# Gate products in fp32r with 256 moving columns a token, four tokens to a block of two weight units, and a reordered early gelu on ScalarE

## The chip, the cores and the metric

One Trainium2 chip, one of its cores. The kernel is a single program with one instruction stream for each engine: TensorE (PE, with its weight loads shown apart as PEld), VectorE (DVE), ScalarE (ACT), GpSimd (POOL) and SyncE (SP). The metric is the device time of one execution in microseconds, the median over several runs.

## The reference

Two blocks of a model on one sequence of 256 tokens with 2048 features, in fp32. The first is an attention and convolution block with a gated embedding. The second is a recurrent branch, a sparse attention branch and then the part that matters here, a layer of 16384 experts (128 by 128 keys):

```python
q = (xf @ wq).reshape(t, PEER_HEADS, PEER_QDIM)
...
top_s, pos = lax.top_k(cand_s, PEER_TOPK)
expert = jnp.take_along_axis(cand_i, pos, axis=-1).reshape(t, -1)
gate = jax.nn.softmax(top_s.astype(jnp.float32), axis=-1).astype(x.dtype).reshape(t, -1)
...
z = jnp.einsum('cd,ced->ce', xc, u[ec])
act = jax.nn.gelu(z, approximate=False) * gc
return jnp.einsum('ce,ced->cd', act, v[ec])
```

Each token picks 128 of the 16384 experts (8 heads, 16 each). The kernel doesn't gather them. It computes z for all experts, multiplies gelu(z) by a gate that is zero where the token didn't pick the expert, and multiplies the result by all of v.

## The kernel before, in words

**Weights in units.** All large weights come in one stream of 904 units of 128 by 1024 fp32 (512 KB), two units to a pair, four buffers (`raw`, `w_hi`, `w_lo`). SyncE loads a unit (L565), ScalarE rounds it to fp32r (`split_hi`, L460), VectorE subtracts to get the rest (`split_lo`, L469). A product is then taken as high times high, high times low and low times high in fp32r. Both splits are written as `ahead(...)`: in the turn of pair p they are made for pair p + 2, and the split of unit u of that pair waits until TensorE has finished unit u of pair p (`unit_done`), because it takes over that unit's buffer.

**A pair of u** (128 experts, one block of z): `halves_out` on TensorE does, for each of the two units, eight matmuls of w_hi with 512 columns (L509, both halves of the activations) and eight of w_lo with 256 columns (L514). The two halves of the bank are then added. Every one of the 128 blocks of z passes through ScalarE's gelu. There are 64 "early" blocks, whose gelu is kept in HBM (`z_kept`) since the gates aren't there yet, and 64 "late" ones.

**Stages of this layer**, in TensorE's order:
- `wqu`, 8 turns of 4 pairs: two of the query projection, two of u. The early blocks go through `early` (L986 to L994) on ScalarE: copy the bank to SBUF (L984), wait until GpSimd has added the halves (L634), gelu (L991), store to `z_kept` (L993).
- `u_decode`, 16 pairs of u, while VectorE works out the picked experts and their gates. At its end three transposes bring the first index, the second index and the gate of each token's 128 picks to partitions (`slot_t`, copied by L1032).
- `u_gates`, 32 pairs of u, with the gate matrix G (second index by first index by token, 128 KB a partition) made between them. For each token, GpSimd writes a one-hot tile of the second index (L655), VectorE one of the first index times the gate (L1787), and TensorE multiplies them in plain fp32 with 128 columns (L2224; the trace holds two matmul records a token). Four tokens follow each unit; ScalarE copies their bank to G (`keep_gates`, L1041). `low_half` (L520) and `add_halves` (L525) put z together, then gelu (L1053) and the store (L1055).
- `u_late`, 64 pairs of u: `low_half`, `add_halves`, gelu (L1071), then on VectorE the gate product of this late block (L1802) and of one early block (L1805) that ScalarE's queue has brought back from `z_kept` (L1064).
- `v`, 128 pairs: 24 matmuls of 512 columns a pair (L2249 to L2251). The expert activations are split two blocks ahead (`expert_hi` L1076, `expert_lo` L1809).

**What sets the order in `u_gates`.** Every engine works through its own instructions in order. On VectorE that order is, for each unit, four tiles (L1787), `split_lo` of one unit, and behind the second unit `add_halves`. On ScalarE: `split_hi` of unit 0, `keep_gates(0)`, `split_hi` of unit 1, `low_half`, `keep_gates(1)`, gelu, store. The tiles are single buffers for each of four tokens, handed back by `hot_used`.

Of the kernel before, what the change touches and what calls it, by code (L numbers as in the profile page):

```python
# [70 lines left out]
         ("wqu", 4 * PH), ("u_decode", 2 * PH), ("u_gates", S // 8), ("u_late", NB // 2), ("v", NB)]  # L71
EARLY = NB // 2
# [11 lines left out]
for _name, _count in [("conv", 4 * CONV_J), ("rnn", 2 * KT), ("heads", 2 * H2), ("u_gates", S // 8),  # L84
                      ("u_late", NB // 2)]:
    HALVED[_name] = _n
    _n += _count
# [46 lines left out]
def build(nc, stream, x, p_t, rows, consts, params, rg_w, ukv, keys_t, out):  # L134
    ctx = ExitStack()
    with ctx:
# [26 lines left out]
        hot = sb("hot", [P, 2, 4, P])  # L163
# [107 lines left out]

        GZ = c("band").rearrange("p (s n) -> p s n", s=2)
# [156 lines left out]
        hot_used = [sem(f"hot_used{n}") for n in range(4)]  # L429
        gate_kept = [sem(f"gate_kept{n}") for n in range(2)]  # L430
# [69 lines left out]
        def halves_out(pe, pair, odd, bank, units=(0, 1), fills=None):  # L500
# [97 lines left out]
        def _(pool):  # L598
# [49 lines left out]
            with pool.Fori(0, S // 8) as i:  # L648
                pool.wait_ge(hot2, i * 8 + 1)
                pool.tensor_copy(idx8, slot_t[:, 1, bass.ds(i * 8, 8)]).then_inc(g_step, 1)  # L650
                pool.wait_ge(g_step, i + 1)
                for s in range(8):
                    pool.wait_ge(hot_used[s % 4], i * 2 + s // 4 + 1)
                    pool.sem_inc(hot_turn, 1)
                    pool.tensor_scalar(hot[:, 1, s % 4, :], iota, idx8[:, s:s + 1], None, ALU.is_equal)\  # L655
                        .then_inc(hot2, 1)
# [9 lines left out]
        def _(act):  # L666
# [319 lines left out]
            def early(pair, b2, n, block, before):  # L986

                copy_halves(Z_HALVES[:, n, :], banks[2 + n], pair, block, before)
                act.wait_ge(z_saved[n], b2 * 16 + 1)
# [7 lines left out]
            with act.Fori(0, PH) as h:  # L997
# [10 lines left out]
                keep_query(0)  # L1008
                ahead(split_hi, act, "wqu", h, 4, 1)
# [3 lines left out]
                early(pair_of("wqu", h, 4, 2), h, 0, h * 4 + 2, 4)  # L1013
                keep_scores(1)
                ahead(split_hi, act, "wqu", h, 4, 3)
                early(pair_of("wqu", h, 4, 3), h, 1, h * 4 + 3, 4)
# [13 lines left out]
            for a in range(3):  # L1030
                act.wait_ge(picks_turned, 2 * a + 2)
                act.activation(slot_t[:, a, :], banks[4 + a][:, 0:S], ACT.Copy).then_inc(slots_kept, 1)  # L1032
            early_turn(PH - 1)
            act.wait_ge(slots_kept, 3)
            act.wait_ge(x_saved, 16)

            with act.Fori(0, S // 16) as i:
                for n in range(2):
                    def keep_gates(m):
                        act.wait_ge(hot_used[3], i * 4 + 2 * n + m + 2)  # L1040
                        act.activation(G[:, :, bass.ds(i * 16 + (8 * n + 4 * m), 4)],  # L1041
                                       banks[m][:, :].rearrange("p (t b) -> p b t", t=4), ACT.Copy)\
                           .then_inc(gate_kept[m], 1)

                    ahead(split_hi, act, "u_gates", i, 2, n, units=(0,))
                    keep_gates(0)
# [4 lines left out]
                    keep_gates(1)  # L1051
# [26 lines left out]
            with act.Fori(0, EARLY // 2 - 1) as i:  # L1078
                late_turn(i)
# [3 lines left out]
            late_turn(EARLY // 2 - 1)  # L1083
            for n in range(2):
                act.wait_ge(act_ready[n], EARLY // 2 + 1)
                act.wait_ge(early_ready[n], EARLY // 2 + 1)
# [5 lines left out]
            with act.Fori(0, NB // 2 - 8) as i:  # L1092
                next_experts(i)
# [47 lines left out]
        def _(dve):  # L1141
# [639 lines left out]
            dve.wait_ge(slots_kept, 3)  # L1781
            with dve.Fori(0, S // 16) as i:
                for n in range(2):
                    for s in range(8):
                        tok = i * 16 + (8 * n + s)
                        dve.wait_ge(hot_used[s % 4], i * 4 + (2 * n + s // 4) + 1)
                        dve.tensor_scalar(hot[:, 0, s % 4, :], iota, slot_t[:, 0, bass.ds(tok, 1)],  # L1787
                                          slot_t[:, 2, bass.ds(tok, 1)], ALU.is_equal, ALU.mult).then_inc(hot1, 1)
                        if s % 4 == 3:
                            ahead(split_lo, dve, "u_gates", i, 2, n, units=(s // 4,))  # L1790
                    add_halves(dve, GZ[:, n, :], banks[2 + n], block_of("u_gates", i, 2, n))
            for n in range(2):
                dve.wait_ge(gate_kept[n], S // 8 + 1)
# [18 lines left out]
            with dve.Fori(0, EARLY // 2 - 1) as i:  # L1812
                late_turn(i)
# [3 lines left out]
            late_turn(EARLY // 2 - 1)  # L1817
            for n in range(2):
                dve.wait_ge(act_ready[n], EARLY // 2 + 1)
                dve.wait_ge(early_ready[n], EARLY // 2 + 1)  # L1820
            with dve.Fori(0, NB // 2 - 2) as i:
                for n in range(2):
                    ahead(split_lo, dve, "v", i, 2, n)
                    expert_lo(i * 2 + (2 + n), n, i * 2 + (3 + n))
# [50 lines left out]
        def _(pe):  # L1875
# [339 lines left out]
            with pe.Fori(0, S // 16) as i:  # L2215
                for n in range(2):
                    pe.wait_ge(gelu_ready[n], i + (2 * PH + 1))
                    for m in range(2):
                        halves_out(pe, pair_of("u_gates", i, 2, n), n, banks[2 + n], units=(m,))
                        pe.wait_ge(gate_kept[m], i * 2 + n + 1)  # L2220
                        for s in range(4):
                            pe.wait_ge(hot1, i * 16 + (8 * n + 4 * m + s + 1))
                            pe.wait_ge(hot2, i * 16 + (8 * n + 4 * m + s + 1) + 1)
                            pe.matmul(banks[m][:, s * P:(s + 1) * P], hot[:, 1, s, :], hot[:, 0, s, :], start=True,  # L2224
                                      stop=True).then_inc(hot_used[s], 1)

            with pe.Fori(0, EARLY // 2) as i:
# [4 lines left out]
            def expert(i, n, first=False):  # L2232
                pe.wait_ge(el_ready, i * 2 + n + 1)
                if first:
                    for m in range(2):
                        pe.wait_ge(gate_kept[m], S // 8 + 1)
                for u in range(2):
                    if first and u == 1:
                        wait_summed(pe, block_of("u_late", EARLY // 2 - 1, 2, 1))
# [159 lines left out]
```

## Time and profile before

| | us |
|---|---|
| median of 3 runs (2788.06 to 2791.62) | 2789.57 |
| the profiled execution, its own time | 2789.84 |
| its span | 2787.9 |
| TensorE matmul busy | 2744.4 |
| TensorE weight loads busy | 2366.5 |
| VectorE busy | 1818.3 |
| ScalarE busy | 1409.1 |
| GpSimd busy | 342.3 |
| mean granted TensorE clock, share of full | 0.996 |

A matmul's record is longer than the time that it adds, since matmuls overlap. So what a group of matmuls costs is read from where one group starts to where the next starts. The same holds for VectorE and ScalarE instructions that follow each other without a wait.

### The profile page before, as it was taken

How to read it: one execution, taken by the hardware profiler on the slowest of the kernel's cores; microseconds unless marked ns; L12 is line 12 of the kernel's file. 1: busy time of each engine (PE TensorE's matmuls, PEld its weight loads, DVE VectorE, ACT ScalarE, POOL GpSimd, SP SyncE). 2: the span in 40 equal slices, each digit the busy share in tenths (PEclk: the TensorE clock that was granted, in tenths of full speed). 3: DMA queues.
4: the chain of work that ended last, by engine and by line, in shares of the span. 5: the costliest groups of instructions: out<-in, count | busy, mean ns of one | idle time of the engine just before them, and what ended most of it. 6: DMA issues, size and time to landing. Idle time of an engine off the chain costs nothing.

```text
span 2787.9 us, 48242 instructions
## 1 busy us (share of the span) xinstructions
PE 2744.4 (98%) x14688; PEld 2366.5 (85%) x14688; DVE 1818.3 (65%) x2903; ACT 1409.1 (51%) x2067; POOL 342.3 (12%) x438
## 2 busy tenths in 40 slices
PE   8999999999999999999999999999999999999998
PEld 6888878888888888888888999888888888888887
DVE  6666665668986666579995666666665555555555
ACT  5455545556665444466655544555554444444444
POOL 0000000000001110011126996000000000000000
PEclk9999999999999999999999999999999999999999
DMA  6544455564554444555555445666665555555564
GB/s 244 190 156 162 150 169 187 177 218 159 173 179 160 158 155 140 195 183 192 191 195 176 156 158 162 214 214 209 214 206 196 195 190 195 192 192 195 191 238 158
DMA packets 153554, 514.76 MB, mean 185 GB/s; under 512 B 17056, under 2 KB 33696, under 8 KB 152480
## 3 DMA queue, kind: packets, MB, share of 16 engines
q1 hardware_dynamic: 131904, 480.44, 52.2%
q10 hardware_dynamic: 21600, 33.70, 3.4%
q8 instruction: 26, 0.43, 0.1%
q14 instruction: 24, 0.20, 0.0%
HBM read 501.49 MB, written 12.58 MB: 184 GB/s over the span
## 4 chain that ended last, share of the span: by engine, by line
PE 73%; issue 21%; POOL 2%; DVE 2%; ACT 1%; DMA 0%; POOLq 0%; SPq 0%; DVEq 0%; ACTq 0%
PE bank L509 21%; PE bank L514 11%; PE bank L2249 8%; PE bank L2251 8%; PE bank L2250 8%; PE bank L547 3%; PE bank L549 3%; PE bank L548 3%; PE bank L2224 2%; POOL big L634 2%; DVE w_lo L469 1%; PE bank L492 1%; PE bank L494 1%; PE bank L493 1%; PE bank L2082 0%
## 5 line engine op out<-in xcount | busy, mean ns | idle before, releaser
L469 DVE TENSOR_TENSOR w_lo<-raw,w_hi 128x1024 fp32r<-128x1024 f32 x904 | 1105.7, 1236 | 796.2 <-ACT w_hi L460 791.0
L460 ACT ACTIVATE w_hi<-raw 128x1024 fp32r<-128x1024 f32 x904 | 951.4, 1059 | 933.0 <-PE bank L2251 373.2
L509 PE MATMUL bank<-act,w_hi 128*128 128x512 f32 x3840 | 980.7, 397 | 5.4 <-ACT big L984 1.9
L509 PEld LDWEIGHTS bank<-act,w_hi 128*128 128x128 f32 x3840 | 692.0, 189 | 136.2 <-issue 7.8
L514 PEld LDWEIGHTS bank<-act,w_lo 128*128 128x128 f32 x3840 | 523.3, 190 | 39.4 <-DVE w_lo L469 0.8
L514 PE MATMUL bank<-act,w_lo 128*128 128x256 f32 x3840 | 535.1, 282 | 0.1
L2249 PE MATMUL bank<-w_hi,expert_act 128*128 128x512 f32 x1008 | 392.2, 389 | 0.1
L2250 PE MATMUL bank<-w_lo,expert_act 128*128 128x512 f32 x1008 | 392.1, 389 | 0.0
L2251 PE MATMUL bank<-w_hi,expert_act 128*128 128x512 f32 x1008 | 392.1, 389 | 0.0
L2249 PEld LDWEIGHTS bank<-w_hi,expert_act 128*128 128x128 f32 x1008 | 189.3, 188 | 39.6 <-DVE cst L525 0.5
L2251 PEld LDWEIGHTS bank<-w_hi,expert_act 128*128 128x128 f32 x1008 | 189.3, 188 | 39.3
L2250 PEld LDWEIGHTS bank<-w_lo,expert_act 128*128 128x128 f32 x1008 | 189.3, 188 | 39.2
L655 POOL TENSOR_SCALAR hot<-cst,stat 128x128 f32<-128x128 f32 x256 | 211.2, 841 | 15.9 <-PE bank L2224 8.7
L661 POOL TENSOR_TENSOR big<-big 128x1024 f32<-128x1024 f32 x2 | 5.8, 2876 | 1051.0 <-DVE big L1836 1051.0
L547 PE MATMUL bank<-w_hi,act 128*128 128x512 f32 x320 | 126.1, 394 | 2.1 <-DVE act L1376 0.9
L548 PE MATMUL bank<-w_lo,act 128*128 128x512 f32 x320 | 125.2, 391 | 0.0
L549 PE MATMUL bank<-w_hi,act 128*128 128x512 f32 x320 | 125.1, 391 | 0.0
L634 POOL TENSOR_TENSOR big<-big 128x256 f32<-128x256 f32 x48 | 61.4, 1280 | 321.6 <-ACT big L984 321.6
L1787 DVE TENSOR_SCALAR hot<-cst,slot_t 128x128 f32<-128x128 f32 x256 | 78.1, 365 | 0.0
L547 PEld LDWEIGHTS bank<-w_hi,act 128*128 128x128 f32 x320 | 60.4, 189 | 16.2 <-DVE w_lo L469 1.5
L1071 ACT ACTIVATE cst<-cst 128x256 f32<-128x256 f32 x64 | 26.8, 419 | 92.7 <-DVE cst L525 92.7
L619 POOL TENSOR_TENSOR big<-big 128x256 f32<-128x256 f32 x16 | 11.2, 699 | 497.3 <-DVE big L525 497.3
(308 smaller groups left out, 2603.3 us busy)
## 6 DMA issues: line engine op xcount, KB each, us to landing
raw<-in_stream SPq DMA_DIRECT2D x904, 512.0 KB, 3.3
big<-in_ukv ACTq DMA_DIRECT2D x16, 512.0 KB, 4.6
z_kept<-cst ACTq DMA_DIRECT2D x64, 128.0 KB, 3.1
cst<-z_kept ACTq DMA_DIRECT2D x64, 128.0 KB, 3.8
big<-in_x SPq DMA_DIRECT2D x2, 1024.0 KB, 9.6
big<-in_rows ACTq DMA_DIRECT2D x2, 1024.0 KB, 8.3
big<-in_rg_w ACTq DMA_DIRECT2D x1, 2048.0 KB, 11.0
x_kept<-big ACTq DMA_DIRECT2D x1, 2048.0 KB, 6.7
```

Of the source, the lines that this page charges most:

```text
L460: act.activation(w_hi[:, s, :], raw[:, s, :], ACT.Copy).then_inc(hi_ready, 1)
L469: dve.tensor_tensor(w_lo[:, s, :], raw[:, s, :], w_hi[:, s, :].bitcast(F32), ALU.subtract).then_inc(lo_ready, 1)
L509: pe.matmul(bank[:, :], w_hi[:, s, kk * P:(kk + 1) * P], act2[:, k, :, :].rearrange("p a n -> p (a n)"), start=(k == 0), stop=False)
L514: mm = pe.matmul(bank[:, 0:S], w_lo[:, s, kk * P:(kk + 1) * P], act_hi[:, k, :], start=False, stop=(k == KT - 1))
L547: pe.matmul(outs[t], a_hi, hi, start=(k == 0), stop=False)
L548: pe.matmul(outs[t], a_hi, lo, start=False, stop=False)
L549: mm = pe.matmul(outs[t], a_lo, hi, start=False, stop=(k == KT - 1))
L634: pool.tensor_tensor(dest, halves[:, 0:S], halves[:, S:2 * S], ALU.add).then_inc(pool_summed, 1)
L655: pool.tensor_scalar(hot[:, 1, s % 4, :], iota, idx8[:, s:s + 1], None, ALU.is_equal)\
L2249: pe.matmul(o, a_hi, hi, start=first, stop=False, skip_group_check=True)
L2250: pe.matmul(o, a_hi, lo, start=False, stop=False, skip_group_check=True)
L2251: mm = pe.matmul(o, a_lo, hi, start=False, stop=False, skip_group_check=True)
```

## The change

- The gate product of a token becomes one fp32r matmul of 256 columns: the one-hot tile of the second index (exact in fp32r) times a tile that holds, side by side, the first index's one-hot times the rounded gate and times the gate's rest. The result is two halves, low and high, which must be added.
- `u_gates` now has 64 pairs and four tokens a pair instead of 32 pairs and eight. `u_late` has 32 pairs instead of 64. So 96 blocks of z are early and 32 late; the 64 early blocks that `u_late` no longer brings back are brought back and multiplied in the first turns of `v`.
- TensorE does the four tokens between the w_hi and the w_lo matmuls of the pair's second unit (`between`).
- VectorE makes the four double tiles first, with one `scalar_tensor_tensor` of 128 by 256 each, then both `split_lo`, then `add_halves`, and then adds the high half of the gates from PSUM onto G, in two instructions of 128 by 256 (`add_gates`).
- ScalarE copies the low half of the gates to G, in two instructions of 128 by 256, between its two `split_hi`.
- In `wqu` and `u_decode` the gelu and the store of an early block (`save_early`) stand behind the splits of the next pair.

```diff
+         ("wqu", 4 * PH), ("u_decode", 2 * PH), ("u_gates", S // 4), ("u_late", NB // 4), ("v", NB)]
+EARLY = 3 * NB // 4
+LATE = NB - EARLY
...
-        hot = sb("hot", [P, 2, 4, P])
+        weighted = sb("weighted", [P, 4, 2, P], F32R)
...
+        GATE_BANKS = [[banks[0], banks[1]], [banks[4], banks[5]]]
...
+                if u and between:
+                    between()
                 pe.wait_ge(lo_ready, 2 * pair + u + 1)
...
             def early_turn(i):
                 for n in range(2):
                     ahead(split_hi, act, "u_decode", i, 2, n)
-                    early(pair_of("u_decode", i, 2, n), i + PH, n, i * 2 + (4 * PH + n), 2)
+                    save_early(i + (PH - 1 + n), 1 - n, i * 2 + (4 * PH + n - 1))
+                    keep_early(pair_of("u_decode", i, 2, n), n, i * 2 + (4 * PH + n), 2)
...
                     ahead(split_hi, act, "u_gates", i, 2, n, units=(0,))
-                    keep_gates(0)
+                    for half in range(2):
+                        act.wait_ge(hot_used[2 * half + 1], i * 2 + n + 2)
+                        act.activation(G[:, :, bass.ds(i * 8 + (4 * n + 2 * half), 2)],
+                                       GATE_BANKS[n][half].rearrange("p (t a b) -> p a b t", t=2, a=2)[:, 1, :, :],
+                                       ACT.Copy).then_inc(gate_low, 1)
                     ahead(split_hi, act, "u_gates", i, 2, n, units=(1,))
...
-                    keep_gates(1)
...
+            with act.Fori(0, (EARLY - LATE) // 2) as i:
+                for n in range(2):
+                    act.wait_ge(early_ready[n], i + (LATE // 2 + 1))
+                    act.dma_start(GB[:, n, :], z_kept[bass.ds(i * 2 + (LATE + n), 1), :, :]
+                                  .rearrange("o p n -> (o p) n")).then_inc(z_back[n], 16)
+                next_experts(i)
...
+            def add_gates(i, n):
+                for half in range(2):
+                    dve.wait_ge(gate_low, i * 4 + (2 * n + half + 1))
+                    dest = G[:, :, bass.ds(i * 8 + (4 * n + 2 * half), 2)]
+                    high = GATE_BANKS[n][half].rearrange("p (t a b) -> p a b t", t=2, a=2)[:, 0, :, :]
+                    dve.tensor_tensor(dest, dest, high, ALU.add).then_inc(gate_kept[n], 1)
+
+            with dve.Fori(0, S // 8) as i:
                 for n in range(2):
-                    for s in range(8):
...
+                    for s in range(4):
+                        tok = i * 8 + (4 * n + s)
+                        dve.wait_ge(hot_used[s], i * 2 + n + 1)
+                        dve.scalar_tensor_tensor(
+                            out=weighted[:, s, :, :], in0=iota.unsqueeze(1).broadcast_to([P, 2, P]),
+                            scalar=first_index[:, bass.ds(tok, 1)],
+                            in1=slot_t[:, 1:3, bass.ds(tok, 1)].broadcast_to([P, 2, P]),
+                            op0=ALU.is_equal, op1=ALU.mult).then_inc(hot1, 1)
+                    ahead(split_lo, dve, "u_gates", i, 2, n)
                     add_halves(dve, GZ[:, n, :], banks[2 + n], block_of("u_gates", i, 2, n))
+                    add_gates(i, n)
...
+            with dve.Fori(0, (EARLY - LATE) // 2) as i:
+                for n in range(2):
+                    next_expert(i, n)
+                    dve.wait_ge(z_back[n], i * 16 + (8 * LATE + 16))
+                    back = G[:, bass.ds(i * 2 + (LATE + n), 1), :].rearrange("p o n -> p (o n)")
+                    dve.tensor_tensor(back, GB[:, n, :], back, ALU.mult).then_inc(early_ready[n], 1)
...
+            def four_tokens(i, n):
+                pe.wait_ge(gate_kept[n], i * 2 + 1)
+                pe.wait_ge(hot1, i * 8 + (4 * n + 4))
+                pe.wait_ge(hot2, i * 8 + (4 * n + 4 + 1))
+                for s in range(4):
+                    pe.matmul(GATE_BANKS[n][s // 2][:, (s % 2) * S:(s % 2 + 1) * S], hot[:, s, :],
+                              weighted[:, s, :, :].rearrange("p a b -> p (a b)"), start=True, stop=True)\
+                      .then_inc(hot_used[s], 1)
+
+            with pe.Fori(0, S // 8) as i:
                 for n in range(2):
                     pe.wait_ge(gelu_ready[n], i + (2 * PH + 1))
...
+                    halves_out(pe, pair_of("u_gates", i, 2, n), n, banks[2 + n], between=lambda: four_tokens(i, n))
```

## Rows read from the trace of the kernel before

**Rows 1.** The page: busy time by engine, and the chain by engine.
```profile
PE 2744.4 (98%) x14688; PEld 2366.5 (85%) x14688; DVE 1818.3 (65%) x2903; ACT 1409.1 (51%) x2067; POOL 342.3 (12%) x438
...
PE 73%; issue 21%; POOL 2%; DVE 2%; ACT 1%; DMA 0%; POOLq 0%; SPq 0%; DVEq 0%; ACTq 0%
```

**Rows 2.** Windows: us, busy by engine, clock, DMA; u_gates, then 32 pairs of u_late.
```profile
1482.24:1725.72 243.48, 240.77 (x1536) 217.47 (x1537) 163.32 (x352) 122.37 (x193) 218.65 (x289) 0.99 0.50 160
1725.72:1904.30 178.58, 178.58 (x1024) 157.12 (x1024) 111.68 (x158) 89.47 (x129) 0.00 (x0) 1.00 0.64 210
```

**Rows 3.** Timeline of TensorE in u_gates: start us, us, engine, line, what.
```profile
1583.32 1.06 PE L2224 MATMUL bank<-hot 128*128 128x128 f32 x8
1584.13 2.09 PE L509 MATMUL bank<-act,w_hi 128*128 128x512 f32 x8
1586.06 1.11 PE L514 MATMUL bank<-act,w_lo 128*128 128x256 f32 x8
```

**Rows 4.** Timeline in u_late, behind the end of a pair.
```profile
1803.09 1.12 PE L514 MATMUL bank<-act,w_lo 128*128 128x256 f32 x8
...
1804.04 2.00 PE L509 MATMUL bank<-act,w_hi 128*128 128x512 f32 x8
...
1804.24 1.06 ACT L460 ACTIVATE w_hi<-raw 128x1024 fp32r<-128x1024 f32 x1 [1.14 <-PE bank L514]
...
1805.42 1.22 DVE L469 TENSOR_TENSOR w_lo<-raw,w_hi 128x1024 fp32r<-128x1024 f32 x1 [0.98 <-ACT w_hi L460]
...
1805.88 1.12 PE L514 MATMUL bank<-act,w_lo 128*128 128x256 f32 x8
1806.57 0.41 DVE L525 TENSOR_TENSOR cst<-cst,bank 128x256 f32<-128x256 f32 x1
...
1806.84 2.00 PE L509 MATMUL bank<-act,w_hi 128*128 128x512 f32 x8
```

**Rows 5.** Timeline in u_gates, VectorE behind add_halves, and the tokens on TensorE.
```profile
1645.45 0.41 DVE L525 TENSOR_TENSOR cst<-cst,bank 128x256 f32<-128x256 f32 x1
...
1645.78 1.23 DVE L1787 TENSOR_SCALAR hot<-cst,slot_t 128x128 f32<-128x128 f32 x4
...
1646.62 1.09 PE L2224 MATMUL bank<-hot 128*128 128x128 f32 x8
```

**Rows 6.** Groups of VectorE by line and shape, and one timeline row of L1640.
```profile
L1582 DVE SCALAR_TENSOR_TENSOR big<-big,par 128x256 f32<-128x256 f32 x48 | 23.3, 485 | 4.2 <-DVE big L1578 1.1 <-DVE big L1582 1.1
...
L1836 DVE TENSOR_TENSOR big<-big,bank 128x512 f32<-128x512 f32 x8 | 5.4, 686 | 1.8 <-PE bank L2269 1.8
...
1009.64 0.87 DVE L1640 SCALAR_TENSOR_TENSOR big<-bank,stat,big 128x256 f32<-128x256 f32 x2
```

**Rows 7.** Groups by line: GpSimd's tiles, ScalarE's gate copies and its plain copies.
```profile
L655 POOL TENSOR_SCALAR hot<-cst,stat 128x128 f32<-128x128 f32 x256 | 211.2, 841 | 15.9 <-PE bank L2224 8.7 <-POOL stat L650 5.3
...
L1041 ACT ACTIVATE big<-bank 128x512 f32 x64 | 37.4, 585 | 1.7 <-PE bank L2224 1.7
...
L984 ACT ACTIVATE big<-bank 128x512 f32<-128x512 f32 x48 | 27.8, 578 | 0.0
```

**Rows 8.** Timeline around TensorE's waits in u_decode and at the start of u_gates.
```profile
1425.53 1.11 PE L514 MATMUL bank<-act,w_lo 128*128 128x256 f32 x8
1428.35 2.11 PE L509 MATMUL bank<-act,w_hi 128*128 128x512 f32 x8 [1.70 <-ACT big L984]
...
1424.66 0.42 ACT L991 ACTIVATE cst<-big 128x256 f32<-128x256 f32 x1 [6.34 <-POOL big L634]
...
1481.67 0.42 ACT L991 ACTIVATE cst<-big 128x256 f32<-128x256 f32 x1 [1.64 <-POOL big L634]
...
1482.24 2.10 PE L509 MATMUL bank<-act,w_hi 128*128 128x512 f32 x8 [1.75 <-ACT cst L991]
```

**Rows 9.** Timeline in v: ScalarE and VectorE between two experts.
```profile
2304.27 1.06 ACT L460 ACTIVATE w_hi<-raw 128x1024 fp32r<-128x1024 f32 x1 [1.35 <-PE bank L2251]
...
2305.45 1.23 DVE L469 TENSOR_TENSOR w_lo<-raw,w_hi 128x1024 fp32r<-128x1024 f32 x1 [1.16 <-ACT w_hi L460]
```

More of the change, by code:

```diff
@@ L83 @@
 _n = 0
-for _name, _count in [("conv", 4 * CONV_J), ("rnn", 2 * KT), ("heads", 2 * H2), ("u_gates", S // 8),
-                      ("u_late", NB // 2)]:
+for _name, _count in [("conv", 4 * CONV_J), ("rnn", 2 * KT), ("heads", 2 * H2), ("u_gates", S // 4),
+                      ("u_late", LATE)]:
     HALVED[_name] = _n
@@ L162, in build @@
             pass
-        hot = sb("hot", [P, 2, 4, P])
+        weighted = sb("weighted", [P, 4, 2, P], F32R)
+        with nc.sbuf_tensor("below_hot", [P, CONST["causal"][0]], F32), \
+                nc.sbuf_tensor("hot", [P, 4, P], F32R) as hot:
+            pass
         cst = sb("cst", [P, CONST_W])
@@ L270, in build @@
         G = big[:, :].rearrange("p (b t) -> p b t", b=NB)
+        first_index = slot_t[:, 0, :]
+        second_index = par[:, 0:S]
+        gate_hi = slot_t[:, 1, :]
+        gate_lo = slot_t[:, 2, :]
+        GATE_BANKS = [[banks[0], banks[1]], [banks[4], banks[5]]]
         GZ = c("band").rearrange("p (s n) -> p s n", s=2)
@@ L498, in block_of, with halves_out @@
             return i * per + (HALVED[part] + k)
-        def halves_out(pe, pair, odd, bank, units=(0, 1), fills=None):
+        def halves_out(pe, pair, odd, bank, units=(0, 1), between=None, fills=None):
             for u in units:
@@ L984, in copy_halves, with keep_early, save_early @@
                 act.activation(dest, bank[:, :], ACT.Copy).then_inc(copied, 1)
-            def early(pair, b2, n, block, before):
+            def keep_early(pair, n, block, before):
                 copy_halves(Z_HALVES[:, n, :], banks[2 + n], pair, block, before)
+            def save_early(b2, n, block):
                 act.wait_ge(z_saved[n], b2 * 16 + 1)
@@ L994, in early, with router_turn @@
                    .then_inc(z_saved[n], 16)
-            with act.Fori(0, PH) as h:
+            def router_turn(h, first=False):
                 def keep_query(a):
@@ L1008, in _ @@
                 keep_query(0)
+                if not first:
+                    save_early(h - 1, 1, (h - 1) * 4 + 3)
                 ahead(split_hi, act, "wqu", h, 4, 1)
@@ L1012, in _ @@
                 ahead(split_hi, act, "wqu", h, 4, 2)
-                early(pair_of("wqu", h, 4, 2), h, 0, h * 4 + 2, 4)
+                keep_early(pair_of("wqu", h, 4, 2), 0, h * 4 + 2, 4)
                 keep_scores(1)
                 ahead(split_hi, act, "wqu", h, 4, 3)
-                early(pair_of("wqu", h, 4, 3), h, 1, h * 4 + 3, 4)
+                save_early(h, 0, h * 4 + 2)
+                keep_early(pair_of("wqu", h, 4, 3), 1, h * 4 + 3, 4)
+            router_turn(0, first=True)
+            with act.Fori(1, PH) as h:
+                router_turn(h)
             def early_turn(i):
@@ L1076, in expert_hi @@
                 act.activation(expert_hi_t[:, n, :], G[:, bass.ds(b, 1), :].rearrange("p o n -> p (o n)"), ACT.Copy)                   .then_inc(eh_ready, 1)
-            with act.Fori(0, EARLY // 2 - 1) as i:
+            with act.Fori(0, LATE // 2 - 1) as i:
                 late_turn(i)
@@ L1778, in _ @@
                 ahead(split_lo, dve, "u_decode", 0, 2, unit // 2, units=(unit % 2,))
-            dve.wait_ge(slots_kept, 3)
-            with dve.Fori(0, S // 16) as i:
-                for n in range(2):
-                    for s in range(8):
[L1785 to L1790, printed above, removed]
+            dve.wait_ge(slots_kept, 4)
+            step(dve.tensor_tensor(gate_lo, gate_lo, gate_hi, ALU.subtract))
+            step.wait()
+            def add_gates(i, n):
[5 more added lines that the diff above has]
+            with dve.Fori(0, S // 8) as i:
+                for n in range(2):
+                    for s in range(4):
[7 more added lines that the diff above has]
+                    ahead(split_lo, dve, "u_gates", i, 2, n)
                     add_halves(dve, GZ[:, n, :], banks[2 + n], block_of("u_gates", i, 2, n))
+                    add_gates(i, n)
             for n in range(2):
-                dve.wait_ge(gate_kept[n], S // 8 + 1)
+                dve.wait_ge(gate_kept[n], S // 4 + 1)
             def late_turn(i):
@@ L1810, in expert_lo @@
                                   expert_hi_t[:, n, :].bitcast(F32), ALU.subtract).then_inc(el_ready, 1)
-            with dve.Fori(0, EARLY // 2 - 1) as i:
+            with dve.Fori(0, LATE // 2 - 1) as i:
                 late_turn(i)
@@ L2213, in _ @@
             decode_turn(PH - 1)
-            with pe.Fori(0, S // 16) as i:
+            def four_tokens(i, n):
[7 more added lines that the diff above has]
+            with pe.Fori(0, S // 8) as i:
                 for n in range(2):
                     pe.wait_ge(gelu_ready[n], i + (2 * PH + 1))
[L2218 to L2227, printed above, removed]
+                    halves_out(pe, pair_of("u_gates", i, 2, n), n, banks[2 + n], between=lambda: four_tokens(i, n))
+            with pe.Fori(0, LATE // 2) as i:
                 for n in range(2):
```

48 lines of the change are left out of this document (24 added, 24 removed).

## The prediction

> **What bounds the kernel now.** I read the page's engine totals first, then the chain of waits, then windows over the stages, then timelines of a few microseconds. The totals and the chain [rows 1] say that TensorE is busy for 98% of the span and that the chain runs through it (PE and its issue hold 94%). So TensorE's own work is the time, unless a change makes it wait. The windows [rows 2] say the same of the two stages that the change re-cuts: u_gates takes 243.48 us for 32 pairs with 256 tokens, and 32 pairs of u_late take 178.58 us, in which TensorE never stops. Together that is 422.1 us for 64 pairs and all gates. This is the quantity that the change moves, since afterwards all 64 pairs stand in u_gates; the other 32 pairs of u_late stay as they are.
>
> In the timelines the starts are to be compared. A unit of u without tokens takes 2.80 us from start to start (1804.04 to 1806.84, [rows 4]): 1.84 for the eight L509, 0.96 for the eight L514, 0.12 each. In u_gates [rows 3] four tokens take 0.81 us (1583.32 to 1584.13) and the L509 behind them 1.93 instead of 1.84, so a unit takes about 3.7.
>
> **TensorE's own part, a gain.** Removed: 64 blocks of four fp32 tokens, 0.81 and the 0.09 behind it, 58 us. Added: 64 blocks of four fp32r matmuls with 256 columns. L514 is the same form, 0.12 each, so 0.48 a block, 31 us. If nothing waits, a pair takes 2 x 2.80 + 0.48 = 6.08 us and 64 pairs 389 us, 33 us less than 422.1.
>
> **VectorE's order, a loss.** What decides is what stands on VectorE between the end of pair p on TensorE and the tokens of pair p + 1. The order there is now: split_lo of the second unit of pair p + 2, add_halves of p, two add_gates of p, and only then the four double tiles of p + 1. The first of these can't start before ScalarE's split_hi, which waits for the end of pair p, because it takes that unit's buffer. So each pair holds a closed chain. I count it from the start of the last eight L514 of pair p:
> - 1.15 to ScalarE's split (1803.09 to 1804.24), 1.18 to VectorE's split (1805.42), 1.15 to add_halves (1806.57) [rows 4];
> - 0.33 to the next instruction (1645.45 to 1645.78) [rows 5];
> - two add_gates, of add_halves' form (128x256, one operand in PSUM), 0.33 each, 0.66;
> - four double tiles. The nearest rows are other scalar_tensor_tensor of 128x256 with a scalar from memory: 485 ns alone (L1582), and two in a row take 0.87, so 0.40 from start to start (L1640) [rows 6]. 3 x 0.40 + 0.485 = 1.69;
> - restart of TensorE: 0.15 from the end of what released it to its matmul (1482.09 to 1482.24) [rows 8];
> - four matmuls, 0.48, and 0.10, by which the first group behind a wait is longer (the L509 at 1482.24 has 2.10 on record against 2.00) [rows 4, 8].
>
> The sum is 6.89 us, and there the next eight L514 start and the chain closes. TensorE alone would need 6.08, so it stands for about 0.8 us in every pair. 64 x 6.89 = 441 us against 422.1: **+19 us**.
>
> Before, the same chain was there and just fitted: behind add_halves stood only four single tiles (1.23 us from 1645.78), no add_gates, and the tokens at 1646.62 waited each for its own tile, not for all four [rows 5].
>
> **Unknown costs, from both sides.** No row shows add_gates, which reads PSUM with a hop at each element and writes G in runs of two. ScalarE's copy of the same pattern costs 585 ns for 128x512 (L1041), 7 ns over a plain copy (L984, 578 [rows 7]), so I take no surcharge. The upper bound is half rate, that is the price of 512 elements, 0.69 less 0.08 overlap (L1836) [rows 6], 0.27 more each, +0.54 a pair. A gain is excluded here: the plain form is the fastest that this shape has. For the double tiles the lower bound is the 0.33 spacing of a plain two-operand instruction, 0.28 less a pair. The restart costs between 0.25 and nothing. So a pair lies between 6.36 and 7.43, and I stay at 6.89, since most of it is read from instructions of the very form.
>
> The VectorE page of the Trainium skill, "Vector Engine (DVE) Microarchitecture Reference", section "Points that are easy to get wrong", speaks against the change: a scalar_tensor_tensor with two non-bf16 operands in SBUF runs at half rate. The row is against that rule here: L1582 has both operands in SBUF in fp32 and takes 485 ns [rows 6], as much as L1640 with one in PSUM, so at about full rate. The sum goes by the row.
>
> **Other engines in the pair.** GpSimd makes four tiles a pair, 841 ns each [rows 7], 3.4 us and about 0.5 for the index copy, starting when the tokens of p are used, 1.5 us before the end of p. It is done about 2.5 us after that end, and the tokens come at 5.3: hidden. It would be the next to be late, from 1.5 us each on. ScalarE has, in a pair, two splits, two copies of 128x256, low_half and gelu, about 3.8 us in 6.9: hidden. Its split of the next pair's unit 0 comes behind gelu and store, and VectorE wants it only behind the double tiles, about when it is ready.
>
> **The early gelu.** Before, GpSimd's slow addition held the gelu back to 1424.66, with the splits and the next copy behind it, and TensorE stood for 1.9 us (1426.49 due, 1428.35 come) [rows 8]. With the splits in front, the copy follows the gelu directly, at about 1425.7, and this wait goes: -1.9. A like one of 0.3 near 1445 goes with it. At the start of u_gates TensorE waits for the last gelu of its bank [rows 8]; that gelu moves behind splits that themselves wait for TensorE, and comes at about 1481.3 instead of 1481.67: -0.4. GpSimd's first tiles then come some 0.5 late: +0.5. Together **-2.1 us**. Elsewhere in wqu and u_decode TensorE didn't wait, so nothing is won there.
>
> **Moved to v.** 64 early blocks are fetched and multiplied there: a DMA issue of 0.35 on ScalarE's queue and 0.43 on VectorE for each of 64 experts. Both engines are idle before every split, 1.35 and 1.16 us [rows 9], and a split has three units of TensorE's work before it is needed. I cost it at nothing. If the cover were gone it would be 64 x 0.78, 50 us at most. The 32 more stores in u_gates hide likewise: DMA is at half its share there [rows 2]. SyncE's queue waits on split_lo, which comes no later than before relative to its use.
>
> **Sum.** 2789.84 (this execution; the median is 0.3 lower) + 19 - 2.1 = about 2806. In general it is 2789.84 - 422.1 - 2.1 + 64 T for a pair of T us. No change would need T = 6.63.
>
> **Rivals.**
> 1. *TensorE stays the bound* and the chain hides, T = 6.08: 2755 us. For it: VectorE has 5.6 us of work in the pair, less than 6.08, so throughput allows it. Against it: the order, which puts all of it but one split behind the end of the pair; the chain would have to be 0.8 us shorter than rows of the same forms say. In this direction lie also T of 6.1 to 6.5, where only the tiles or the restart are cheaper. Together 0.20, a result below 2784.
> 2. *add_gates is slow.* From a surcharge of 0.27 us each on, T is 7.43 and the time 2841. For it: the hop at each element in PSUM. Against it: L1041. It is a worse form of my forecast, 0.12.
> 3. *Double tiles at half rate*, as if 512 elements: 0.27 more for each of four, T = 7.97, 2876 us. Against it stands L1582. 0.03. (This is what the rule of the Trainium skill's page named above would do here.)
> 4. *v loses its cover*: ScalarE waits for VectorE's early product before it splits, and this from over 8 us on delays TensorE. 0.03, up to +50.
> 5. *The change doesn't do what it says*, a wait elsewhere dominates: covered by the ends.
>
> **How the numbers follow.** My forecast has 0.62, the rivals the rest. The range takes in T from 6.36 to 7.43, that is 2773 to 2841; outside lie the full form of rival 1 and rivals 3 and 4. A measurement of this kernel tells about 0.2%, 5.6 us, from no change: that is T within 6.54 to 6.71. Slower by more: 0.70. Within: 0.10. Faster by more: 0.20.
>
> **What would show it.** In the profile of the changed kernel, TensorE's idle time before the gate matmul, released by VectorE's tiles, of about 0.8 us, 64 times, some 50 us in all; from one block of tokens to the next 6.9 us; granted clock still near 1.0; four gate matmuls 0.5 us; scalar_tensor_tensor at 480 to 500 ns and add_gates at 410. TensorE's busy time falls by about 30 us while the span grows. The wait on L984 near 1428 is gone. The forecast is wrong if the blocks follow at 6.1 us, or if the releaser is GpSimd or ScalarE.

## The result and the profile after

The changed kernel takes 2810.59 us, median of 4 runs (2810.03 to 2811.20), against 2789.69: ratio 1.0072, 95% interval 1.0060 to 1.0084. It is slower, as forecast, by 20.9 us; the sum of the forecast was +19 and -2.1, about 17 (2806). Its profiled execution took 2810.31 us with a span of 2808.5. The kernel before was measured again beside the experiments: 2789.68 us beside e1 to e4, and 2791.46 beside e1b, e5, e7 and e8 (the median without one slow run of 3911.68), so times of these two groups differ by up to 2 us for no cause in the kernel.

First the page of the changed kernel, its engine totals, its chain by line, and the gate matmul, the double tile and GpSimd's tile among the groups.

```profile
PE 2729.5 (97%) x14432; PEld 2331.9 (83%) x14432; DVE 1878.5 (67%) x3032; ACT 1404.2 (50%) x2117; POOL 342.4 (12%) x438
...
PE bank L519 12%; PE bank L526 9%; PE bank L2302 8%; PE bank L2304 8%; PE bank L2303 8%; DVE weighted L1825 4%; PE bank L559 3%; PE bank L560 3%; PE bank L561 3%; ACT w_hi L470 3%; PE bank L2271 2%; DVE big L1818 1%; POOL big L646 1%; DVE w_lo L479 1%; PE bank L502 1%
...
L667 POOL TENSOR_SCALAR hot<-cst,stat 128x128 fp32r<-128x128 f32 x256 | 212.8, 847 | 210.7 <-PE bank L2271 210.4
...
L1825 DVE SCALAR_TENSOR_TENSOR weighted<-cst,slot_t 128x256 fp32r<-128x256 f32 x256 | 106.2, 474 | 0.4 <-DVE slot_t L1811 0.4
...
L2271 PE MATMUL bank<-weighted,hot 128*128 128x256 f32 x256 | 47.1, 306 | 36.2 <-DVE weighted L1825 35.0
```

TensorE has 15 us less of matmul records than before (2729.5 against 2744.4) and the span is 21 us longer. The chain, which in the kernel before was nearly all TensorE [rows 1], now holds the double tiles (L1825, 4%), ScalarE's split (L470, 3%) and add_gates (L1818, 1%). The gate matmul is the group on TensorE that waits longest by far: 36.2 us, 35.0 of them for the double tiles.

The windows of the changed kernel over u_gates, u_late and v give the whole difference. Columns are as in [rows 2].

```profile
1483.10:1924.14 441.04, 404.80 (x2304) 340.22 (x2305) 322.84 (x574) 223.22 (x383) 220.68 (x289) 1.00 0.53 171
1924.14:2103.88 179.74, 179.03 (x1026) 157.38 (x1025) 113.55 (x162) 90.14 (x130) 0.00 (x0) 1.00 0.64 210
2103.88:2808.00 704.12, 696.81 (x3074) 576.32 (x3072) 383.74 (x464) 317.44 (x404) 5.75 (x2) 1.00 0.62 206
```

The same cuts of the kernel before, u_late and v:

```profile
1725.72:2083.38 357.66, 357.66 (x2051) 314.75 (x2051) 226.07 (x320) 179.96 (x259) 0.00 (x0) 1.00 0.64 211
2083.38:2787.50 704.12, 696.79 (x3074) 576.50 (x3072) 362.94 (x400) 317.53 (x404) 5.75 (x2) 1.00 0.58 194
```

- u_gates with its 64 pairs takes 441.04 us. The same pairs took 243.48 [rows 2] and half of 357.66, together 422.31: **+18.7**.
- u_late takes 179.74 for 32 pairs against 178.83: +0.9.
- v takes 704.12 in both, with all its added fetches and products.
- u_gates begins at 1483.10 instead of 1482.24 [rows 8]: +0.9. The four add up to the 20.5 between the profiled executions.

The timeline of one pair in the changed kernel answers to [rows 3 to 5]:

```profile
1702.49 0.74 PE L2271 MATMUL bank<-weighted,hot 128*128 128x256 f32 x4 [0.56 <-DVE weighted L1825]
...
1703.07 1.12 PE L526 MATMUL bank<-act,w_lo 128*128 128x256 f32 x8
...
1704.22 1.06 ACT L470 ACTIVATE w_hi<-raw 128x1024 fp32r<-128x1024 f32 x1 [0.41 <-PE bank L526]
...
1705.41 1.23 DVE L479 TENSOR_TENSOR w_lo<-raw,w_hi 128x1024 fp32r<-128x1024 f32 x1 [1.83 <-ACT w_hi L470]
...
1706.55 0.41 DVE L537 TENSOR_TENSOR cst<-cst,bank 128x256 f32<-128x256 f32 x1
...
1706.88 0.78 DVE L1818 TENSOR_TENSOR big<-big,bank 128x256 f32 x2
...
1707.58 1.66 DVE L1825 SCALAR_TENSOR_TENSOR weighted<-cst,slot_t 128x256 fp32r<-128x256 f32 x4
...
1709.37 0.74 PE L2271 MATMUL bank<-weighted,hot 128*128 128x256 f32 x4 [0.55 <-DVE weighted L1825]
```

Read by its starts, this is the closed chain: the last w_lo matmuls of a pair (1703.07), ScalarE's split after 1.15, VectorE's after 1.19, add_halves after 1.14, add_gates after 0.33, the tiles after 0.70, the gate matmuls after 1.79. The next w_lo matmuls follow after 0.57. From one block of tokens to the next it is 6.88 us.

### The profile page after: what moved, and what is told of

It is laid out like the page before. It is cut to its first block, busy times and chain, and to the rows that moved or that the text cites. A ratio compares the mean times of both kernels' runs of the same rounds, so it can differ in the third digit from the quotient of the medians.

```text
span 2808.5 us, 48261 instructions
## 1 busy us (share of the span) xinstructions
PE 2729.5 (97%) x14432; PEld 2331.9 (83%) x14432; DVE 1878.5 (67%) x3032; ACT 1404.2 (50%) x2117; POOL 342.4 (12%) x438
## 4 chain that ended last, share of the span: by engine, by line
PE 62%; issue 24%; DVE 7%; ACT 3%; POOL 2%; DVEq 1%; DMA 0%; POOLq 0%; ACTq 0%; SPq 0%
PE bank L519 12%; PE bank L526 9%; PE bank L2302 8%; PE bank L2304 8%; PE bank L2303 8%; DVE weighted L1825 4%; PE bank L559 3%; PE bank L560 3%; PE bank L561 3%; ACT w_hi L470 3%; PE bank L2271 2%; DVE big L1818 1%; POOL big L646 1%; DVE w_lo L479 1%; PE bank L502 1%
## 5 line engine op out<-in xcount | busy, mean ns | idle before, releaser
L470 ACT ACTIVATE w_hi<-raw 128x1024 fp32r<-128x1024 f32 x904 | 953.4, 1059 | 919.2 <-PE bank L2304 294.4
L667 POOL TENSOR_SCALAR hot<-cst,stat 128x128 fp32r<-128x128 f32 x256 | 212.8, 847 | 210.7 <-PE bank L2271 210.4
L1825 DVE SCALAR_TENSOR_TENSOR weighted<-cst,slot_t 128x256 fp32r<-128x256 f32 x256 | 106.2, 474 | 0.4 <-DVE slot_t L1811 0.4
L646 POOL TENSOR_TENSOR big<-big 128x256 f32<-128x256 f32 x48 | 58.6, 1222 | 322.8 <-ACT big L996 322.8
L2271 PEld LDWEIGHTS bank<-weighted,hot 128*128 128x128 f32 x256 | 34.1, 188 | 62.9 <-issue 61.3
L2271 PE MATMUL bank<-weighted,hot 128*128 128x256 f32 x256 | 47.1, 306 | 36.2 <-DVE weighted L1825 35.0
```

Source lines behind the costliest of these rows:

```text
L470: act.activation(w_hi[:, s, :], raw[:, s, :], ACT.Copy).then_inc(hi_ready, 1)
L667: pool.tensor_scalar(hot[:, s % 4, :], iota, idx8[:, s:s + 1], None, ALU.is_equal)\
L1825: dve.scalar_tensor_tensor(out=weighted[:, s, :, :], in0=iota.unsqueeze(1).broadcast_to([P, 2, P]), scalar=first_index[:, bass.ds(tok, 1)] ...
```

## The experiments

Eight kernels ran, all made from the changed kernel. Three change VectorE's order in u_gates, two add a tile there, one changes a wait on TensorE, and two are about the early gelu. `tiles` holds the loop over four double tiles of the changed kernel, unchanged, for the pair that it is given. Ratios are against the kernel before.

**e1: the tiles of the next pair first, as soon as this pair's tokens are used.**

```diff
-            with dve.Fori(0, S // 8) as i:
+            tiles(0, 0)
+            with dve.Fori(0, S // 8 - 1) as i:
                 for n in range(2):
-                    for s in range(4):
...
+                    tiles(i, n + 1)
                     ahead(split_lo, dve, "u_gates", i, 2, n)
                     add_halves(dve, GZ[:, n, :], banks[2 + n], block_of("u_gates", i, 2, n))
                     add_gates(i, n)
```

> The changed kernel, with the four double tiles of the next pair made on VectorE as soon as the tokens of this pair are used, ahead of this pair's two splits. Theory (order, not work): nothing but the splits, add_halves and add_gates is left behind the end of a pair, none of which TensorE's next tokens need, so a pair falls from 6.88 to 6.08 us and the time from 2810 to about 2759. Rival (VectorE has too much work): the pair still has the same instructions, 5.6 us of them with little slack, so a pair stays at 6.6 or more and the time above 2790. Rival (GpSimd next): tokens wait for the one-hot tiles, idle time before the gate matmul released by GpSimd.

Measured: 2760.12 us, ratio 0.9894 (0.9878 to 0.9911). The timeline of e1, over one pair:

```profile
1701.20 0.64 PE L2280 MATMUL bank<-weighted,hot 128*128 128x256 f32 x4
...
1705.68 0.41 DVE L537 TENSOR_TENSOR cst<-cst,bank 128x256 f32<-128x256 f32 x1
1706.01 0.78 DVE L1818 TENSOR_TENSOR big<-big,bank 128x256 f32 x2
...
1707.26 0.64 PE L2280 MATMUL bank<-weighted,hot 128*128 128x256 f32 x4
...
1707.80 1.81 DVE L1824 SCALAR_TENSOR_TENSOR weighted<-cst,slot_t 128x256 fp32r<-128x256 f32 x4 [1.01 <-PE bank L2280]
```

The blocks follow at 6.06 us and no idle time stands before them. VectorE now waits for TensorE (1.01 us) and not the reverse. The instructions are the same as in the changed kernel and the time is 50 us shorter, so the loss lay in the order alone. With this order the change as a whole is 29.6 us faster than the kernel before; what the fp32r product gives by itself was not measured. GpSimd's tiles are slower here (305.5 us for 256, 1209 ns each, against 847), but four of them fit in the pair: the second rival is out.

**e2: only add_gates moved behind the next tiles.**

```diff
+                    add_gates(i, n - 1)
                     ahead(split_lo, dve, "u_gates", i, 2, n)
                     add_halves(dve, GZ[:, n, :], banks[2 + n], block_of("u_gates", i, 2, n))
-                    add_gates(i, n)
```

> The changed kernel, with only add_gates of a pair moved behind the four double tiles of the next pair. Theory (closed chain): exactly the two add_gates, 0.70 us from start to start, leave the chain; a pair goes from 6.88 to 6.18 us and the time from 2810 to about 2765. Rival (VectorE's work as such bounds the pair): the same instructions in another order, no change, 2810.

Measured: 2771.49 us, ratio 0.9930 (0.9913 to 0.9947). The rival is out. From the first to the last block of tokens it is 6.24 us a pair, 0.64 of the 0.70 gained; the time is 6.5 us above what was expected. The 0.06 a pair make 3.8 of these, and in the traces e2 is already 1.7 us behind the changed kernel when `wqu` begins (1202.71 against 1201.00), ahead of everything that the edit touches. The timeline of e2 shows a pair of 6.18 us, as counted, and ahead of it a split_lo of 1.33 us instead of 1.23, as every second one there:

```profile
1699.87 1.33 DVE L479 TENSOR_TENSOR w_lo<-raw,w_hi 128x1024 fp32r<-128x1024 f32 x1 [1.13 <-ACT w_hi L470]
...
1703.25 0.74 PE L2280 MATMUL bank<-weighted,hot 128*128 128x256 f32 x4
...
1709.43 0.73 PE L2280 MATMUL bank<-weighted,hot 128*128 128x256 f32 x4
```

Why every second split is longer wasn't tried.

**e3: each gate matmul waits for its own tile.**

```diff
-                pe.wait_ge(hot1, i * 8 + (4 * n + 4))
...
                 for s in range(4):
+                    pe.wait_ge(hot1, i * 8 + (4 * n + s + 1))
```

> The changed kernel, with each gate matmul waiting for its own double tile and not for all four. Theory: tiles come every 0.40 us, so three of the four matmuls are done when the last tile comes, and only one, 0.12, is left of the 0.57 us between the first gate matmul and the next w_lo matmul; a pair loses 0.35 to 0.45 us and the time goes to 2782 to 2788. If the wait is for another thing than the tiles: no change, 2810.

Measured: 2787.66 us, ratio 0.9992 (0.9983 to 1.0002): the kernel before and this one can't be told apart. A pair takes 6.50 us, 0.38 less. So what TensorE waits for is the last of the four tiles, and three of the matmuls hide behind the making of the others.

**e4: a fifth double tile in every pair.**

```diff
                         dve.wait_ge(hot_used[s], i * 2 + n + 1)
+                        if s == 0:
+                            dve.scalar_tensor_tensor(
+                                out=banks[7][:, 0:S].rearrange("p (a b) -> p a b", a=2),
...
```

> The changed kernel, with a fifth scalar_tensor_tensor of the same shape in every pair, in front of the four, its result written to an unused PSUM bank. Theory: it lies on the closed chain, so a pair grows by its spacing, 0.35 to 0.42 us, and the time by 22 to 27 us, to about 2835. If the chain had slack the time would stay within 5 us of 2810.

Measured: 2835.35 us, ratio 1.0164 (1.0147 to 1.0181), 24.8 us above the changed kernel, 0.39 a pair. TensorE's idle time before the gate matmuls goes from 0.55 to 0.95 us (timeline of e4):

```profile
1706.26 0.73 PE L2277 MATMUL bank<-weighted,hot 128*128 128x256 f32 x4 [0.95 <-DVE weighted L1831]
```

**e7: the same fifth tile in e1.** The diff is that of e4 on top of e1.

> e1 (tiles of the next pair ahead of the splits) with the fifth tile of e4 in every pair. Theory: with the tiles off the chain VectorE has 0.8 to 1.0 us of idle time a pair, so 0.40 more of work hides: 2758 to 2763. Rival (VectorE's amount of work bounds e1): plus 20 us or more.

Measured: 2760.64 us, ratio 0.9888 (0.9872 to 0.9903), the time of e1. The same instruction costs 25 us in one order and nothing in the other. The groups on VectorE in us 1500 to 1870 show where it went, in e1 and then in e7:

```profile
L1824 DVE SCALAR_TENSOR_TENSOR weighted<-cst,slot_t 128x256 fp32r<-128x256 f32 x244 | 110.8, 512 | 54.7 <-PE bank L2280 54.7
```

```profile
L1825 DVE SCALAR_TENSOR_TENSOR bank<-cst,slot_t 128x256 f32<-128x256 f32 x61 | 33.3, 546 | 29.5 <-PE bank L2286 29.5
```

VectorE's idle time in front of the tiles falls from 54.7 to 29.5 us in these 61 pairs, and that pays for the tile.

**e1b: the tiles of the next pair between the two splits.**

```diff
+                    ahead(split_lo, dve, "u_gates", i, 2, n, units=(0,))
+                    tiles(i, n + 1)
+                    ahead(split_lo, dve, "u_gates", i, 2, n, units=(1,))
```

> As e1 (tiles of the next pair made early), but standing between this pair's two splits on VectorE and not ahead of both. TensorE's tokens still wait for nothing behind the end of their pair. Theory (the chain of the order, counted from rows): a second closed chain opens between VectorE and ScalarE that does not touch TensorE: split of unit 1, 1.15, add_halves 0.41, gelu and its store on ScalarE 1.08, ScalarE's next split to VectorE's 1.18, split of unit 0, 1.15, four tiles 1.60, together 6.57 us a pair, so about 2760 + 64 x 0.50 = 2792. Rival (only TensorE's tokens matter): as e1, 2760.

Measured: 2800.59 us, ratio 1.0036 (1.0024 to 1.0049). The loop between VectorE and ScalarE is there, and it holds TensorE: in this kernel TensorE waits for ScalarE's gelu, which hands back the bank (58 times, 13.3 us by the records). Timelines of e1b, VectorE, then ScalarE, then one row of TensorE:

```profile
1704.29 1.23 DVE L479 TENSOR_TENSOR w_lo<-raw,w_hi 128x1024 fp32r<-128x1024 f32 x1 [1.90 <-ACT w_hi L470]
1705.43 1.66 DVE L1824 SCALAR_TENSOR_TENSOR weighted<-cst,slot_t 128x256 fp32r<-128x256 f32 x4
1707.01 1.22 DVE L479 TENSOR_TENSOR w_lo<-raw,w_hi 128x1024 fp32r<-128x1024 f32 x1
1708.15 0.41 DVE L537 TENSOR_TENSOR cst<-cst,bank 128x256 f32<-128x256 f32 x1
...
1710.83 1.23 DVE L479 TENSOR_TENSOR w_lo<-raw,w_hi 128x1024 fp32r<-128x1024 f32 x1 [1.59 <-ACT w_hi L470]
```

```profile
1703.10 1.06 ACT L470 ACTIVATE w_hi<-raw 128x1024 fp32r<-128x1024 f32 x1 [0.94 <-ACT cst L1073]
...
1708.59 0.42 ACT L1073 ACTIVATE cst<-cst 128x256 f32<-128x256 f32 x1 [2.67 <-DVE cst L537]
...
1709.65 1.06 ACT L470 ACTIVATE w_hi<-raw 128x1024 fp32r<-128x1024 f32 x1 [0.64 <-ACT cst L1073]
```

```profile
1709.17 2.10 PE L519 MATMUL bank<-act,w_hi 128*128 128x512 f32 x8 [0.25 <-ACT cst L1073]
```

The pair at 1704.29 closes at 1710.83, 6.54 us, as counted (6.57). But every second pass takes 0.3 more, since ScalarE's next split then comes 0.94 and not 0.64 us behind the gelu. From first to last block it is 6.65 us, which makes 5 of the 8.6 us above what was expected. Some 3 more are at the start of `u_late`, where TensorE waits 3.0 us for add_halves and its clock then falls for a few microseconds. So it is not enough that TensorE's next tokens wait for nothing behind the end of their pair: of the two places tried for the tiles, only the one ahead of both splits frees TensorE.

**e5: the early gelu back in its old place, in the changed kernel.**

```diff
-                    save_early(i + (PH - 1 + n), 1 - n, i * 2 + (4 * PH + n - 1))
                     keep_early(pair_of("u_decode", i, 2, n), n, i * 2 + (4 * PH + n), 2)
+                    save_early(i + PH, n, i * 2 + (4 * PH + n))
```

(and the same in wqu)

> The changed kernel with the early gelu and its store in their old place, directly behind the copy of their block and ahead of the next splits. Theory: the new place is a small loss, since splits that come earlier keep VectorE busy without a pause and GpSimd's addition in the decode stage then takes 8.4 us instead of 6.2; undone, TensorE's longest wait in that stage falls from 3.5 to about 1.9 us and the time by 1 to 3 us, to about 2808. Rival (the new place is a gain, as predicted, and something else made the wait longer): the time grows by about 2 us, to 2812 or more.

Measured: 2814.81 us, ratio 1.0081 (1.0067 to 1.0095). That is 4.2 us above the changed kernel, but the two weren't measured side by side: by their ratios it is 2.5 us, and the intervals overlap. The traces are clearer. The profiled execution of e5 is 4.7 us longer, and 1.9 of these are there when `wqu` begins (1202.89 us against 1201.00), ahead of everything that the edit touches. The rest, 2.8 us, belongs to the edit, and it is a loss where my theory had a gain. The waits on TensorE are, in e5:

```profile
1429.99 2.11 PE L519 MATMUL bank<-act,w_hi 128*128 128x512 f32 x8 [1.70 <-ACT big L996]
...
1484.22 2.11 PE L519 MATMUL bank<-act,w_hi 128*128 128x512 f32 x8 [2.07 <-ACT cst L1006]
...
1493.22 0.73 PE L2269 MATMUL bank<-weighted,hot 128*128 128x256 f32 x4 [4.11 <-POOL hot L667]
```

and in the changed kernel:

```profile
1435.44 2.11 PE L519 MATMUL bank<-act,w_hi 128*128 128x512 f32 x8 [3.45 <-ACT big L996]
...
1483.10 2.10 PE L519 MATMUL bank<-act,w_hi 128*128 128x512 f32 x8 [1.61 <-ACT cst L1006]
...
1489.23 0.73 PE L2271 MATMUL bank<-weighted,hot 128*128 128x256 f32 x4 [1.25 <-POOL hot L667]
```

The first wait did behave as expected, 1.70 against 3.45, and the new place loses there. Counted from the start of `wqu`, its net loss up to the start of `u_gates` is 0.8 us. But it wins 2.9 us at the first tokens: ScalarE's last copy follows the gelu directly, where in e5 two splits stand between them, so GpSimd begins its last addition at 1484.10 and not 1487.11, and its first tiles early. The clock behind that wait (last section) adds 0.8 us at the second block of tokens. So in this kernel the reorder is a gain of about 3 us by the traces, made of a loss and a larger gain at places that I hadn't costed.

**e8: e1, with a pause on VectorE in the decode stage.**

```diff
                     unit = next(lows)
+                    if unit >= 2 and unit % 2 == 0:
+                        dve.wait_ge(pool_summed, 4 * PH + unit // 2 + 4)
                     ahead(split_lo, dve, "u_decode", 0, 2, unit // 2, units=(unit % 2,))
```

> e1, and in the decode stage VectorE waits, ahead of the first split of each pair of u, until GpSimd has added the halves of the block before. Theory: GpSimd's addition is slow there because VectorE gives it no pause; with a pause it takes 0.7 to 2 us everywhere, TensorE's wait of 3.5 us in that stage falls below 1 us, and the time falls by 2 to 4 us, to about 2757. Rival (GpSimd's addition is slow by itself, or TensorE then waits for the splits instead): the wait stays or moves, 2760 or more.

Measured: 2756.06 us, ratio 0.9875 (0.9859 to 0.9890), 4.1 us below e1, the fastest here, and 35.4 us below the kernel before as it ran beside it. In the traces `wqu` begins at the same time in both to 0.1 us, and `u_gates` at 1479.48 instead of 1483.37, so the gain is where the edit is. GpSimd's additions around the wait, in e1 and then in e8:

```profile
1418.30 5.32 POOL L646 TENSOR_TENSOR big<-big 128x256 f32<-128x256 f32 x1 [4.88 <-ACT big L996]
1425.43 8.38 POOL L646 TENSOR_TENSOR big<-big 128x256 f32<-128x256 f32 x1 [1.81 <-ACT big L996]
1435.65 0.74 POOL L646 TENSOR_TENSOR big<-big 128x256 f32<-128x256 f32 x1 [1.84 <-ACT big L996]
```

```profile
1418.22 4.18 POOL L646 TENSOR_TENSOR big<-big 128x256 f32<-128x256 f32 x1 [4.87 <-ACT big L996]
1424.21 0.74 POOL L646 TENSOR_TENSOR big<-big 128x256 f32<-128x256 f32 x1 [1.81 <-ACT big L996]
1429.39 1.53 POOL L646 TENSOR_TENSOR big<-big 128x256 f32<-128x256 f32 x1 [4.44 <-ACT big L996]
```

The addition of 8.38 us becomes one of 0.74, and TensorE's wait of 3.45 us in that stage is gone. Single additions of 4.2 and 3.3 us remain, so "0.7 to 2 everywhere" was too good.

## Why the prediction was right, point by point

- **The closed chain** was the whole matter, and it holds. I counted 6.89 us a pair from rows of the kernel before; measured are 6.88. That the sum is so close is part luck, since single terms are off by up to 0.05 and cancel. Term by term: 1.15, 1.18, 1.15 came as 1.15, 1.19, 1.14; two add_gates 0.66 as 0.70; the tiles and the restart 1.84 as 1.79; the gate matmuls 0.58 as 0.57. e2, e3 and e4 each change one term and move the pair by 0.64, 0.38 and 0.39 us, where the chain says 0.70, 0.35 to 0.45 and 0.35 to 0.42.
- **TensorE's own part**, 6.08 us a pair if nothing waits: e1 has 6.07. Rival 1 named this kernel's time as 2755, and e1, which gives TensorE this freedom, has 2760. As a forecast for the change it was rightly put below the chain. The prediction gives TensorE's gain twice, though, and the two don't agree: 58 less 31 is 27 us, and 422.1 less 389 is 33. Of the 6 us between them 5 are at the first tokens of the kernel before. They were due at 1485.13 and came at 1487.91, after GpSimd's tiles, and they and the L509 behind them then took 4.93 us (to 1492.84) instead of 2.74, at the lower clock (last section). That is no price of the fp32 product.
- **+19 us for u_gates**: 18.7.
- **Unknown costs.** add_gates takes 0.78 us for two, 0.35 each from start to start; the hop in PSUM costs next to nothing, and rival 2 is out. The double tiles take 474 ns, the price of L1582 and L1640, so rival 3 is out. By the rule of the Trainium skill ("Vector Engine (DVE) Microarchitecture Reference", "Points that are easy to get wrong") a scalar_tensor_tensor with two fp32 operands in SBUF would run at half rate; the trace of the changed kernel disagrees: 474 ns, 256 times, no more than L1640's 477 with one operand in PSUM.
- **v loses nothing**: 704.12 us before and after, so rival 4 is out.
- **Idle time** was foretold as some 50 us before the gate matmuls. The trace puts 36.2 us in front of the gate matmul. A matmul's record reaches beyond the start of the next, so records hide a part of each wait; by starts it is 6.88 - 6.07 (e1) = 0.81 us a pair, 52 us. For the same reason TensorE's busy time fell by 15 us and not by the 30 foretold: the records cover some 16 us of waiting.
- **The early gelu, -2.1 us, failed in its parts.** The step wanted the start of u_gates 2.6 us earlier than before (1.9, 0.3 and 0.4) and the first tokens 0.5 late. The wait near 1428 did go, but one of 3.6 us (1431.83 due, 1435.44 come) stands at the next pair. I had taken GpSimd's addition as given and moved only what stands behind it. In the kernel before, VectorE idles for 2.8 us ahead of 1426.81 and GpSimd's next addition takes 0.73 us; with the splits first, VectorE works without a pause, and that addition takes 8.4 us (e8 gives VectorE a pause, and the wait goes). The small wait near 1445 stayed at 0.3, and u_gates began at 1483.10, 0.9 later than before instead of 2.6 earlier. At the first tokens the sign was wrong too: e5 shows that the new place makes GpSimd's first tiles earlier. Against e5 the reorder is worth some 2.8 us, so if -2.1 looks right as a net figure, that is luck.
- **What is missing in the sum.** Unrounded it gives 2806.6 us for the profiled execution, which took 2810.3, 3.7 more. The start of u_gates is 3.5 of that, and a wait in u_late that I didn't have is 0.9: there TensorE's third pair waits (1935.32 due, 1936.18 come) for add_halves of the stage's first block. Its splits start on ScalarE 8.0 us behind the start of the stage (6.8 before), after the store of the last early block, which here comes 3.6 us into the stage instead of 2.7. u_gates itself, with its first tokens, is 0.6 below the sum.

The changed kernel's other moves weren't tried alone: the shift of 32 blocks from u_late to u_gates, and the fp32r product itself, are in every kernel here but the one before.

## What to carry to other kernels

An engine's share of busy time doesn't say whether it holds others up: VectorE was busy for 73% of u_gates in the changed kernel (322.84 of 441.04 us) and set its pace. Look for what must happen between the end of one turn and the first need in the next; if an in-order engine has unrelated work queued in between, add it up from starts to starts. Such a sum, made of rows of the kernel before, was good to 0.01 us in 6.9 here, and its single terms to 0.05. And the cure is a reordering: put what the next turn needs in front of what waits for the end of this one (50 us here, with the same instructions).

## What the runs showed of the hardware that was not expected

- **GpSimd's addition stretches with VectorE's work.** In the changed kernel an addition of two 128x256 fp32 operands takes 0.73 us at 1438.88, beside a VectorE reduction, and 8.39 us from 1425.15 to 1433.54, while VectorE runs two-operand instructions back to back until 1432.95 and then idles. It ends 0.6 us after VectorE stops. The addition ahead of it (5.32 us from 1418.02) ended 0.7 us after VectorE had gone over from two-operand instructions to a reduction (L1790, at 1422.66). Timelines of the changed kernel, GpSimd and then VectorE:

```profile
1425.15 8.39 POOL L646 TENSOR_TENSOR big<-big 128x256 f32<-128x256 f32 x1 [1.81 <-ACT big L996]
```

```profile
1431.67 1.28 DVE L1785 TENSOR_TENSOR big<-big 128x512 f32<-128x512 f32 x2
1436.28 1.23 DVE L479 TENSOR_TENSOR w_lo<-raw,w_hi 128x1024 fp32r<-128x1024 f32 x1 [3.33 <-ACT w_hi L470]
```

  The Trainium skill ("SBUF — State Buffer", "SBUF: two separate sides") says that VectorE, when it has two inputs in SBUF, and a GpSimd instruction that reads SBUF share a pair of ports, and that whichever starts first locks it for its whole instruction while the other blocks. The trace agrees that GpSimd stands still beside such instructions. It disagrees on who wins: VectorE's instructions that began after 1425.15 ran at their usual times (1.21 us a split), one after another, and GpSimd, which had begun before them, lost to several in a row.
- **TensorE's clock can fall behind a wait.** Windows of the kernel before, ahead of and behind its first tokens, and of e5 ahead of and behind the end of its wait of 4.1 us (granted clock is the third column from the right):

```profile
1482.00:1488.00 6.00, 3.14 (x17) 2.61 (x17) 3.79 (x6) 3.14 (x6) 2.50 (x4) 1.00 0.78 268
1488.00:1492.60 4.60, 4.51 (x15) 3.69 (x16) 2.54 (x5) 1.51 (x2) 4.60 (x7) 0.63 0.68 193
```

```profile
1484.00:1493.20 9.20, 4.90 (x24) 3.88 (x24) 6.18 (x8) 4.03 (x6) 5.68 (x6) 1.00 0.69 224
1493.20:1498.20 5.00, 4.98 (x21) 4.40 (x22) 1.43 (x2) 2.00 (x4) 2.53 (x5) 0.66 0.32 108
```

  In both, TensorE had been busy for about half of the stretch ahead (3.14 of 6.00 us, 4.90 of 9.20), and then most of the next 5 us ran at 1.2 instead of 2.4 GHz. In the changed kernel, with a wait of 1.25 us at this place, the clock stays at 1.00, and the 64 waits of about 0.8 us cost it nothing. The dip is part of what the gelu's new place saves: from the first block of tokens to the second e5 takes 7.71 us and the changed kernel 6.87.

  A wait doesn't always bring it, even the same one. Windows behind TensorE's wait of 3.45 us in the decode stage, in the changed kernel and in e7, whose code there is the same:

```profile
1435.40:1440.40 5.00, 4.96 (x26) 4.29 (x27) 4.12 (x3) 4.26 (x6) 1.45 (x2) 1.00 0.35 103
```

```profile
1436.00:1442.00 6.00, 5.47 (x17) 4.71 (x18) 4.63 (x4) 5.25 (x8) 1.47 (x2) 0.50 0.38 131
```

  So a few microseconds between two profiled executions can be such dips, and a small difference is better read from the stage that an edit touches than from the whole time.
